# Two-block transformer step on one core: attention results and projected queries transposed by VectorE squares and small transfers instead of TensorE

## What is computed

```python
q = (rmsnorm(q_lat, q_norm_g[l]) @ w_uq[l]).reshape(b, s, MLA_HEADS, QK_HEAD_DIM)      # 8 heads, 128 plain + 64 rotated
q = jnp.concatenate([q[..., :QK_NOPE_DIM],
                     apply_rope(q[..., QK_NOPE_DIM:], cos[:, :, None, :], sin[:, :, None, :])], axis=-1)
a_out = mla_attention(q, k, v)                                                         # softmax(q k) v
m_out = memory_attention(q_mem.reshape(b, s, MEM_HEADS, MEM_HEAD_DIM), mem_n, w_mk[l], w_mv[l])   # 4 heads
y = jnp.concatenate([a_out, c_out, m_out], axis=-1) * jax.nn.silu(gate)
o = y @ w_o[l]
```

## Time and profile before

| | |
|---|---|
| median of 3 runs | 2307.06 us (2307.02 to 2307.28) |
| the profiled execution | 2307.33 us |
| its span, first to last instruction | 2305.5 us |
| PE busy | 2294.6 us of it, 10829 matmuls |
| DVE busy | 1463.2 us (63%), 1969 instructions |
| ACT busy | 1173.9 us (51%), 1549 instructions |
| TensorE clock granted, mean | 0.999 of full speed |
| DMA | 443.08 MB, mean 192 GB/s |

### The profile page before, as it was taken

How to read it: one execution, slowest core, us unless ns; L and a number is a source line. 1 busy time by engine, 2 the same in 40 slices (tenths; PEclk the granted TensorE clock), 3 DMA queues, 4 the chain that set the end, 5 groups by cost and what they waited for, 6 DMA issues and landing times.

```text
span 2305.5 us, 27392 instructions
## 1 busy us (share of the span) xinstructions
PE 2294.6 (100%) x10829; PEld 1925.8 (84%) x10829; DVE 1463.2 (63%) x1969; ACT 1173.9 (51%) x1549; POOL 25.5 (1%) x35
## 2 busy tenths in 40 slices
PE   9999999999999999999999999999999999999998
PEld 7888888888888888888888888888888888888887
DVE  6677777756666666676467566675555755565565
ACT  6555655444445744444444444465655446565443
...
GB/s 295 179 190 200 195 186 168 225 202 202 193 206 267 175 195 196 192 193 195 188 199 192 193 191 217 228 167 195 157 158 157 212 216 147 204 157 156 159 202 136
DMA packets 243983, 443.08 MB, mean 192 GB/s; under 512 B 18736, under 2 KB 48944, under 8 KB 243216
## 3 DMA queue, kind: packets, MB, share of 16 engines
...
## 4 chain that ended last, share of the span: by engine, by line
PE 98%; DVE 1%; ACT 0%; DMA 0%; SPq 0%; issue 0%; DVEq 0%; ACTq 0%
PE pm L997 30%; PE pm L999 30%; PE pm L998 30%; PE pb L654 2%; PE pb L836 1%; PE pb L734 1%; PE pb L744 0%; DMA raw<-in_w_in 0%; DVE wl L2192 0%; PE pb L818 0%; PE pb L816 0%; PE pm L991 0%; PE pm L992 0%; PE pm L986 0%; PE pb L817 0%; PE pm L990 0%
## 5 line engine op out<-in xcount | busy, mean ns | idle before, releaser
L2192 DVE TENSOR_TENSOR wl<-raw,wh 128x1024 fp32r<-128x1024 f32 (+3 forms) x786 | 948.6, 1211 | 717.6 <-ACT wh L1501 714.6
L1501 ACT ACTIVATE wh<-raw 128x1024 fp32r<-128x1024 f32 (+3 forms) x786 | 819.8, 1046 | 909.0 <-PE pm L999 904.7
L997 PE MATMUL pm<-wh,hTh 128*128 128x512 f32 x702 | 275.5, 392 | 1.4 <-DVE wl L2192 1.3
L998 PE MATMUL pm<-wl,x2Th 128*128 128x512 f32 x704 | 274.2, 389 | 0.0
L999 PE MATMUL pm<-wh,x2Tl 128*128 128x512 f32 x704 | 274.2, 389 | 0.0
L997 PE MATMUL pm<-wh,x2Th 128*128 128x512 f32 x704 | 274.1, 389 | 0.0
L999 PE MATMUL pm<-wh,hTl 128*128 128x512 f32 x702 | 273.6, 390 | 0.0
L998 PE MATMUL pm<-wl,hTh 128*128 128x512 f32 x702 | 273.6, 390 | 0.0
L997 PE MATMUL pm<-wh,xT3h 128*128 128x512 f32 (+1 forms) x640 | 251.2, 392 | 0.0
L999 PE MATMUL pm<-wh,xT3l 128*128 128x512 f32 (+1 forms) x640 | 245.1, 383 | 0.0
L998 PE MATMUL pm<-wl,xT3h 128*128 128x512 f32 (+1 forms) x640 | 244.8, 382 | 0.0
...
## 6 DMA issues: line engine op xcount, KB each, us to landing
...
```

The lines of the kernel that those rows point to most:

```text
L997: e.matmul(o, ah[:, kk, t], h[:, c], start=first, stop=False)
L998: e.matmul(o, ah[:, kk, t], l[:, c], start=False, stop=False)
L1501: e.activation(h[:, 0:n], r[:, 0:n], ACT.Copy).then_inc(s["hi"], 1)
L2192: e.tensor_tensor(l[:, 0:n], r[:, 0:n], h[:, 0:n].bitcast(F32), ALU.subtract).then_inc(s["lo"], 1)
```

## The change

In rounds 0 to 4 of each layer the results are no longer transposed by PE. They lie in one tile `PP`, and 16 VectorE instructions on 32 partitions each (`results_turned`, due at part 2 plus 2 to plus 5) put the transposed squares into `yR`, from where ACT and DVE make the two parts of `yT` with one instruction each. Round 5, a layer's last two heads, stays on PE. `uq_turn` and `uqr_turn` are gone: `uq_rope` transposes the plain part within squares into `uqZ`, rotates, and transposes the rotated part into `uqZ` too. SP issues 16 transfers for each of the four groups, 24 KB each, into `uqR`, due from the group's end plus 5 to plus 12. ACT copies to `qT` and `qTr` due at the group's end plus 20, and DVE makes the low parts due at plus 22. All four groups uq now land in `S2[0]`.

```diff
 ROUNDS = ((56, 60, 63, 69), (70, 74, 77, 81), (96, 100, 103, 107), (118, 122, 125, 129), (140, 144, 147, 151),
           (158, 162, 165, 169))
-UQ_N, UQ_R = (71, 91, 113, 135), (79, 95, 117, 139)
...
+            for j in range(4):
+                for n in range(16):
+                    if n % 2 == 0:
+                        yield p.end[f"uq{l}{j}"] + 5 + n // 2
+                    w.wait_ge(s["uz"], 4 * l + j + 1)
+                    w.wait_ge(s["uzr"], 4 * l + j + 1)
+                    w.wait_ge(s["uq_l"], 4 * l + j)
+                    w.wait_ge(s["uqr_l"], 2 * (4 * l + j))
+                    a_, c = n // 4, n % 4
+                    e.dma_start(m.uqR[l][32 * c:32 * c + 32, a_, :, :, :], m.uqZ[32 * a_:32 * a_ + 32, c, :, :, :]
+                                ).then_inc(s["d_uq"], 16)
...
-        if which == 3:
+        if which == 3 and r == 5:
             for ln in range(2):
                 free(6 + ln)
                 w.wait_ge(s["ys"], 2 * (idx + ln) + 2)
                 turn(6 + ln, 0, [m.P[ln][:, qh, 0:128] for qh in range(2)]).then_inc(s["yt_t"], 1)
-                bank[6 + ln] = ("y_l", idx + ln + 1)
...
-    def uq_turn(l, j):
-        S = m.S2[S2_OF[f"uq{j}"]]
-        free(6)
-        w.wait_ge(s["ev_a"], p.evac[f"uq{l}{j}"])
-        for f in range(2):
-            ins = turn(6, f, [S[:, half, f * 192:f * 192 + 128] for half in range(2)])
-        ins.then_inc(s["uq_t"], 1)
-        bank[6] = ("uq_l", 4 * l + j + 1)
-
-    def uqr_turn(l, j):
-        free(7)
-        w.wait_ge(s["rp"], RP[f"uq{l}{j}"])
-        turn(7, 0, [m.rope_o[:, half, :] for half in range(2)]).then_inc(s["uqr_t"], 1)
-        bank[7] = ("uqr_l", 2 * (4 * l + j + 1))
+                bank[6 + ln] = ("y_l", 7 * l + r + ln + 1)
...
-                if r == 1 and which == 0:
-                    yield L + UQ_N[0]
-                    uq_turn(l, 0)
-                if r == 1 and which == 2:
-                    yield L + UQ_R[0]
-                    uqr_turn(l, 0)
-        yield L + UQ_N[1]
-        uq_turn(l, 1)
-        yield L + UQ_R[1]
-        uqr_turn(l, 1)
...
-        if which == 1:
+        if which == 1 and r < 5:
+            k = 12 + 2 * r if r < 2 else 2 * (r - 2)
+            w.wait_ge(s["yt_t"], 7 * l + r + 1)
+            e.activation(m.yT[0][:, k:k + 2, :], m.yR[:, :, :], ACT.Copy).then_inc(s["y_h"], 1)
+        elif which == 1:
             for ln in range(2):
-                k = 12 + 2 * r + ln if r < 2 else 2 * (r - 2) + ln
-                if k in (6, 7):
-                    w.wait_ge(s["mm"], p.end[f"ukv{l}3"])
-                w.wait_ge(s["yt_t"], idx + ln + 1)
-                e.activation(m.yT[0][:, k:k + 1, :], view(6 + ln, 1), ACT.Copy).then_inc(s["y_h"], 1)
```

`uq_turn` and `uqr_turn` are also taken out of the later rounds of PE's `layer`. On ACT, SP and DVE:

```diff
     def uq_copy(l, j):
-        w.wait_ge(s["uq_t"], 4 * l + j + 1)
+        w.wait_ge(s["d_uq"], 256 * (4 * l + j + 1))
         if j >= 2:
             w.wait_ge(s["sc"], 12 * l + 2 * j + 2)
-        e.activation(m.qT[j % 2][0][:, :, :], view(6), ACT.Copy).then_inc(s["uq_c"], 1)
+        e.activation(m.qT[j % 2][0][:, :, :].rearrange("p f (h a t) -> p f h a t", h=2, a=4),
+                     m.uqR[l][:, :, 0:2, :, :].rearrange("p a f h t -> p f h a t"), ACT.Copy).then_inc(s["uq_c"], 1)
...
-        yield L + ROUNDS[0][3] + 1
+        yield L + ROUNDS[0][2] + 7
         attention(l, 0, 1)
         yield L + ROUNDS[1][0] + 2
         attention(l, 1, 0)
-        uq_copy(l, 0)
-        yield L + UQ_R[0] + 1
-        uqr_copy(l, 0)
-        yield L + ROUNDS[1][3] + 1
+        yield L + ROUNDS[1][2] + 7
         attention(l, 1, 1)
...
-            yield L + ROUNDS[rr][3] + 1
+            yield L + ROUNDS[rr][2] + 7 if rr < 5 else L + ROUNDS[rr][3] + 1
             attention(l, rr, 1)
             if rr < 4:
                 yield p.end[f"uq{l}{rr}"]
                 uq_taken(l, rr)
             if rr < 5:
+                yield p.end[f"uq{l}{rr - 1}"] + 20
+                uq_copy(l, rr - 1)
+                uqr_copy(l, rr - 1)
+            if rr < 5:
                 yield p.end[f"ukv{l}{rr - 1}"]
                 ukv_taken(l, rr - 1)
...
+        if which == 4 and r < 5:
+            k = 12 + 2 * r if r < 2 else 2 * (r - 2)
+            w.wait_ge(s["y_h"], 7 * l + r + 1)
+            e.tensor_tensor(m.yT[1][:, k:k + 2, :], m.yR[:, :, :], m.yT[0][:, k:k + 2, :].bitcast(F32), ALU.subtract
+                            ).then_inc(s["y_l"], 1)
+
+    def results_turned(l, r, at0):
+
+        yield at0
+        w.wait_ge(s["ys"], 2 * (2 * (6 * l + r) + 2))
+        for a in range(4):
+            yield at0 + a
+            for c in range(4):
+                ins = e.transpose(m.yR[32 * c:32 * c + 32, :, :].rearrange("p n (h a t) -> p n h a t", h=2, a=4)[:, :, :, a, :],
+                                  m.PP[32 * a:32 * a + 32, :, :, 32 * c:32 * c + 32])
+        ins.then_inc(s["yt_t"], 1)
...
         S = m.S2[S2_OF[f"uq{j}"]][:, :, 0:384].rearrange("p a (h d) -> p a h d", h=2)
         O = m.rope_o[:, :, :].rearrange("p a (h d) -> p a h d", h=2)
         w.wait_ge(s["ev_a"], p.evac[f"uq{l}{j}"])
+        w.wait_ge(s["kv_t"], l + 1)
         if l or j:
-            w.wait_ge(s["uqr_t"], 4 * l + j)
+            w.wait_ge(s["d_uq"], 256 * (4 * l + j))
+            w.wait_ge(s["uzr"], 4 * l + j)
+        e.transpose(m.uqZ[:, :, 0:2, :, :].rearrange("p r f h t -> p f h r t"),
+                    m.S2[0][:, :, 0:384].rearrange("p h (f d) -> p f h d", f=2)[:, :, :, 0:128]
+                    .rearrange("p f h (r c) -> p f h r c", c=32)).then_inc(s["uz"], 1)
         rope((S[:, :, :, 128:160], S[:, :, :, 160:192]), (O[:, :, :, 0:32], O[:, :, :, 32:64]), 2, RP[f"uq{l}{j}"] - 6)
+        w.wait_ge(s["rp"], RP[f"uq{l}{j}"])
+        e.transpose(m.uqZ[:, :, 2, :, :].rearrange("p r h t -> p h r t"),
+                    m.rope_o[:, :, :].rearrange("p h (r c) -> p h r c", c=32)).then_inc(s["uzr"], 1)
...
+            if r < 5:
+                yield from results_turned(l, r, three + 2)
...
+            yield three + 8 if r < 5 else four + 1
             attention(l, r, 4)
             if 1 <= r <= 3:
                 yield p.end[f"uq{l}{r}"]
                 uq_rope(l, r)
-                yield L + UQ_N[r] + 1
-                uq_low(l, r)
+            if 1 <= r <= 4:
+                yield p.end[f"uq{l}{r - 1}"] + 22
+                uq_low(l, r - 1)
+                uqr_low(l, r - 1)
```

More of the change, by code:

```diff
@@ L246 @@
           (158, 162, 165, 169))
[L247 to L248 removed]
+S2_OF = {"ql": 0, "kv": 1, "qm": 0, "uq0": 0, "uq1": 0, "uq2": 0, "uq3": 0, "gc": 0}
 SEMAPHORES = """mm hi lo ev_a ev_d nh sq st_r st_v rstd scl sq0 warm xsq xrd xss msq mrd mss hT_h hT_l pool_m wp_h wp_l dT_h dT paT_h paT_l gu g_h la_m la_d la_a zq zo d_zq d_zo
@@ L365, in buffers @@
     m.S2 = [at(f"s2{i}", [128, 2, 512], RC + 60 + 4 * i) for i in range(2)]
-    m.P = [at("P0", [128, 2, T], 4.5), at("P1", [128, 2, T], 6.5)]
+    m.PP = at("PP", [128, 2, 2, T], 4.5)
+    m.P = [m.PP[:, ln, :, :] for ln in range(2)]
     m.PT = [at("PT0", [128, 2, T], 8.5), at("PT1", [128, 2, T], 216)]
+    m.yR = at("yR", [128, 2, T], 2.5)
+    m.uqZ = at("uqZ", [128, 4, 3, 2, 32], RC + 64)
+    m.uqR = [at(f"uqR{l}", [128, 4, 3, 2, 32], (208, 200)[l]) for l in range(2)]
     m.kpeT = halves("kpeT", 1, 10.5, 218)
@@ L458, in ready @@
     r, ln = ((k - 12) // 2, k % 2) if k >= 12 else (2 + k // 2, k % 2)
-    return "y_l", 12 * layer + 2 * r + ln + 1
+    return "y_l", 7 * layer + r + 1 + (r == 5 and ln)
 def sync_program(nc, s, m, a, cst, cpool, gains, out, p):
@@ L1097, in attention @@
                                  scale=scale, accum_out=ls[:, qh:qh + 1]).then_inc(s["ex"], 1)
-        if which == 1:
-            for ln in range(2):
-                k = 12 + 2 * r + ln if r < 2 else 2 * (r - 2) + ln
-                if k in (6, 7):
-                    w.wait_ge(s["mm"], p.end[f"ukv{l}3"])
-                w.wait_ge(s["yt_t"], idx + ln + 1)
-                e.activation(m.yT[0][:, k:k + 1, :], view(6 + ln, 1), ACT.Copy).then_inc(s["y_h"], 1)
+        if which == 1 and r < 5:
[3 more added lines that the diff above has]
+        elif which == 1:
+            for ln in range(2):
+                w.wait_ge(s["mm"], p.end[f"ukv{l}3"])
+                w.wait_ge(s["yt_t"], 7 * l + r + ln + 1)
+                e.activation(m.yT[0][:, 6 + ln:7 + ln, :], view(6 + ln, 1), ACT.Copy).then_inc(s["y_h"], 1)
     def uq_taken(l, j):
         key = f"uq{j}"
-        before = {"uq0": ("kv_t", l + 1), "uq1": ("qm_t", 2 * l + 2), "uq2": ("uq_t", 4 * l + 2),
-                  "uq3": ("uq_t", 4 * l + 3)}[key]
-        roped = {"uq0": f"kv{l}", "uq1": f"kv{l}", "uq2": f"uq{l}1", "uq3": f"uq{l}2"}[key]
+        before = ("uz", 4 * l + j) if j else ("qm_t", 2 * l + 2)
+        roped = f"uq{l}{j - 1}" if j else f"kv{l}"
         w.wait_ge(s["rstd"], RS[f"ql{l}"])
@@ L1757, in attention @@
                                            ).then_inc(s["ys"], 1)
-            if which == 4:
```

(19 more changed lines are left out.)

47 lines of the change are left out of this document (11 added, 36 removed).

## The result

| | before | after |
|---|---|---|
| median | 2307.11 us (2307.02 to 2307.28) | 2337.28 us (2336.22 to 2338.64) |
| span of the profiled execution | 2305.5 us | 2336.7 us |
| mean granted clock | 0.999 | 0.994 |

The change makes the kernel slower by 1.3%: ratio 1.0131, 95% interval 1.0113 to 1.0149. That is the predicted sign and inside the predicted range, 8.6 us above the predicted 2328.7 and at the upper edge of the forecast's own range (2316 to 2337). What follows splits those 30.2 us.

The account below looks back on a forecast made before the run. PE's chain, 98% of the span, was taken as the bound: 2307.33 - 9.6 spared + 31.2 of stalls = 2328.9, less 0.27 to the median gives 2328.7 us. Range 2308 to 2341 us.

Parts of the forecast that it names:

- What bounds it: Whole kernel: 98% of the span is PE, so work PE no longer executes comes off unless something it awaits comes later.
- What PE is spared: PE, both layers: 88 transposes gone at 0.109 us each, saving 9.6 us.
- Transposes of 0.30 us with a pitch of 0.31: DVE: each new 128-element transpose takes 0.30 us, 0.31 with spacing; sixteen take 4.96 us a round.
- The rival with cheap transposes: DVE: new transposes cost about 0.18 us, stalls total 14.4 us, time 2312 us; chance 0.16.
- Place 1: Round 1's exponentials: DVE's added work makes PE stall 5.0 us before transposing the probabilities, in each layer.
- From the first maximum to the last exponential: Round 1's exponentials: this stretch takes 2.85 us, putting the last exponential at 1648.00.
- Places 2 and 3: Scores of rounds 3 and 4: PE stalls 3.2 us each per layer, partly earlier at gc's first matmul.
- Place 4: Scores of round 5: PE stalls 4.2 us per layer, waiting for DVE's low part of the keys.
- The sum of the waits: Both layers: 2 x (5.0 + 3.2 + 3.2 + 4.2) = 31.2 us of PE stalls.
- Transfers cost nothing: SP's 16 transfers per group: land at 1761 against ACT's copy at 1773.5, cover 12 us, no cost.
- The rival on the clock: Behind the longer stalls PE's clock falls to half; 2333 us or 2337 us; chance 0.18.
- Two falls: Clock drops behind long stalls, each losing 2.1 us: two give 2333 us, four 2337 us.

Follow-up runs that it names:

- kernel with queries alone: Changed kernel with all results transposed by PE again, only queries going by squares and transfers; 2301.34 us, ratio 0.9975 to the kernel before.
- the last experiment: Changed kernel reordered: result transposes stay early, high and low parts of rounds 1 to 4 behind keys' parts, round 1 and queries' work moved; 2299.78 us, ratio 0.9967.

## Why the prediction was right, and where it was off

- **What bounds it** held: PE's chain, and waits that stand where none had stood.
- **What PE is spared**: 88 transposes, at 0.12 us each by the kernel with queries alone, against the 0.109 used.
- **Transposes of 0.30 us with a pitch of 0.31**: measured 303 ns, and eight in 2.51 us as worked out from the earlier trace rows. The squares were put at 0.70 and 0.44, measured 0.706 and 0.445. The rival with cheap transposes falls.
- **Place 1, stall 5.0**: measured 4.2, twice. DVE's row was right: the sum put the first maximum at 1645.15, it came at 1644.88. The step that was off is "From the first maximum to the last exponential": PE's first four transposes need only the first head's exponentials, and it started at 1646.88, before the last one at 1647.52.
- **Places 2 and 3, 3.2 each**: measured 1.68 + 1.41 and 1.68 + 1.46, split as predicted between the first matmul of the group that needs the PSUM of `s` and the keys' low part. The path was the predicted one: from the last transpose (1745.12 in round 3) over ACT to its high part took 3.95 us where the sum had 4.07, and from there to the end of `kT0l` (1756.55) 7.48 where it had 7.51. The runs add what of it could be moved: the readers of the transposes, not the transposes.
- **Place 4, 4.2**: measured 4.4.
- **The sum of the waits**, 31.2, was 29.6. **Transfers cost nothing** held: their median landing was 2.9 us and ACT never waited for them in the changed kernel.
- **The rival on the clock** came true, which the forecast had at nothing. Two falls give 2333, four 2337, it said; there were four, at 9.2 us in all instead of 8.4, and 2337.3. Its ground was the earlier trace rows, a wait of this length that had lost the clock; that was the better reading, and with 0.18 I had it too low. That its 2337 was met so closely is in part luck. Its waits were 1.6 us too long, the term of the next point was missing in it, and its 2.1 us a fall came from nine matmuls at the start: for these the profile's granted clock reads 1.00, so that only their pitch of 0.46 us speaks for the low level, and behind the four waits a fall cost 1.7 to 2.7 us. The Trainium skill's warning that pauses between bursts of matmuls bring the lower clock (TensorE: Matmul & The Clock Gate, Why this matters for your kernels) agrees with the windows (0.50 behind these four waits), and the runs that kept PE busy show the waits as the cause of the low clock.
- **A term that was missing**: a wait costs more than its idle time. At place 1, the last matmul before it starts at 1642.28 and a next one would have started at 1642.51, but its record ends at 1642.67, from where the idle time counts. That is 0.16 us for each of 12 waits, 1.9 us.

The account for the profiled execution: -9.6 spared, +29.6 waits, +9.2 clock, +1.9 ends of matmuls, -0.6 for waits for the stream's parts (0.7 after, 1.3 before): +30.5, of 31.2 in the spans. The rest of 0.7 us is open.

What the prediction did not see is how little of this belonged to the work itself. It named what stands behind the transposes in DVE's row, and took the order as given; the last experiment shows that the same instructions leave PE only 1.4 us of new waits once the readers of the transposes in rounds 1 to 3 stand behind what PE needs, and that these 1.4 us hang on the one in round 4 that does not.
